# First stage of a conditioned decoder block: c spread by TensorE, whole W_ada rows, single k tiles, last tile split

## The reference

```
mod  = silu(c) @ W_ada + b_ada            # W_ada 2048 x 12288: shift1, scale1, gate1, shift2, scale2, gate2
h    = rms_norm(x, w1) * (1 + scale1) + shift1
proj = h @ W_in                           # 16 heads: 8 retention (q, k, v, gate), 8 differential (q, k, v)
...                                       # heads, W_out, second norm, MLP of width 8192, final norm
```

## Time and profile before

| | |
|---|---|
| median of 3 runs | 2376.55 us |
| the profiled execution's own time | 2377.6 us |
| its span | 2375.3 us |
| TensorE products busy | 2311.1 us, 97% |
| DVE busy | 1265.9 us, 53% |
| ScalarE busy | 751.4 us, 32% |
| GpSimd busy | 76.9 us, 3% |
| DMA queue of SP | 326.41 MB, 39.4% of 16 engines |
| mean granted clock of TensorE | 0.995 |

### The profile page before, as it was taken

The page is one execution under the profiler, slowest core; times in us unless marked ns, Lnnn a source line. Parts: engine busy times, 40 slices in busy tenths (PEclk is TensorE's granted clock), DMA queues, the critical chain, the costliest instruction groups (busy, mean ns, idle before and its releaser), DMA issues.

```text
span 2375.3 us, 28446 instructions
## 1 busy us (share of the span) xinstructions
PE 2311.1 (97%) x10328; PEld 1880.7 (79%) x10328; DVE 1265.9 (53%) x1797; ACT 751.4 (32%) x1020; POOL 76.9 (3%) x58
## 2 busy tenths in 40 slices
PE   4999999999999999999999999999999999999997
PEld 3568888878887788888888888888888888888886
DVE  7977988867676675733333333333333333333344
ACT  3233343354545422421221221221322222222332
POOL 0011110100101000000000000000000000000000
PEclk9999999999999999999999999999999999999998
DMA  9956677722222574232222222222222222222222
GB/s 377 399 204 221 230 266 248 250 94 80 80 80 79 187 275 159 86 101 97 98 98 97 93 101 96 94 95 96 97 97 97 97 97 96 99 97 95 90 95 92
DMA packets 90630, 328.25 MB, mean 138 GB/s; under 512 B 10064, under 2 KB 10576, under 8 KB 89936
## 3 DMA queue, kind: packets, MB, share of 16 engines
q1 hardware_dynamic: 89568, 326.41, 39.4%
q10 hardware_dynamic: 1008, 1.13, 0.2%
HBM read 323.31 MB, written 4.19 MB: 138 GB/s over the span
## 4 chain that ended last, share of the span: by engine, by line
issue 60%; PE 28%; DVE 9%; ACT 2%; DMA 1%; POOL 0%; SPq 0%; DVEq 0%; POOLq 0%; ACTq 0%
PE bank L436 8%; PE bank L440 8%; PE bank L437 8%; DVE ada_sb L1001 3%; DVE w_lo L994 2%; PE bank L577 1%; DVE prob L1001 1%; PE bank L543 1%; PE bank L460 1%; DMA xy<-x_t 1%; PE bank L568 0%; DMA prob<-ada 0%; ACT w_hi L719 0%; ACT L812 0%; DVE hf L1034 0%
## 5 line engine op out<-in xcount | busy, mean ns | idle before, releaser
L436 PE MATMUL bank<-act_hi,w_hi 128*128 128x512 f32 (+1 forms) x2112 | 829.5, 393 | 13.2 <-DVE act_lo L1041 4.6
L437 PE MATMUL bank<-act_lo,w_hi 128*128 128x512 f32 (+1 forms) x2112 | 820.2, 389 | 0.0
L719 ACT ACTIVATE w_hi<-raw 128x1024 fp32r<-128x1024 f32 x392 | 413.8, 1056 | 895.5 <-PE bank L440 841.6
L994 DVE TENSOR_TENSOR w_lo<-raw,w_hi 128x1024 fp32r<-128x1024 f32 x392 | 492.0, 1257 | 309.0 <-ACT w_hi L719 296.1
L440 PE MATMUL bank<-act_hi,w_lo 128*128 128x512 f32 (+1 forms) x2112 | 518.3, 387 | 0.0
L436 PEld LDWEIGHTS bank<-act_hi,w_hi 128*128 128x128 f32 x2112 | 398.1, 188 | 101.6 <-issue 17.7
L437 PEld LDWEIGHTS bank<-act_lo,w_hi 128*128 128x128 f32 x2112 | 398.1, 189 | 81.9 <-issue 1.7
L440 PEld LDWEIGHTS bank<-act_hi,w_lo 128*128 128x128 f32 x2112 | 394.5, 188 | 81.1
L436 PE MATMUL bank<-u_hi,w_hi 128*128 128x512 f32 x1024 | 399.9, 390 | 0.0
L437 PE MATMUL bank<-u_lo,w_hi 128*128 128x512 f32 x1024 | 398.6, 389 | 0.0
L1396 DVE SCALAR_TENSOR_TENSOR xy<-bank,modr,xy 128x512 f32 (+1 forms) x143 | 107.4, 751 | 418.7 <-PE bank L440 418.7
(11 more groups left out here) (140 smaller groups left out, 1115.0 us busy)
## 6 DMA issues: line engine op xcount, KB each, us to landing
raw<-weights SPq DMA_DIRECT2D x400, 512.0 KB, 3.2
ada_sb<-ada SPq DMA_DIRECT2D x172, 512.0 KB, 5.3
prob<-ada SPq DMA_DIRECT2D x20, 512.0 KB, 6.8
xy<-x_t SPq DMA_DIRECT2D x16, 512.0 KB, 6.0
out<-rows_out SPq DMA_DIRECT2D x4, 1024.0 KB, 5.9
decay_sb<-decay SPq DMA_DIRECT2D x7, 256.0 KB, 2.8
silu_c<-c_row SPq DMA_DIRECT2D x1, 1024.0 KB, 5.6
rot_sb<-rot ACTq DMA_DIRECT2D x2, 256.0 KB, 7.0
```

What stands on the lines that cost most here:

```text
L436: pe.matmul(acc, stationary, hi, start=first, stop=False)
L437: pe.matmul(acc, stationary, lo, start=False, stop=False)
L719: nc.scalar.activation(w_hi[:, w], raw[:, r], ACT.Copy).then_inc(hi_ready, 1)
L994: nc.vector.tensor_tensor(w_lo[:, w], raw[:, r], w_hi[:, w].bitcast(F32), ALU.subtract).then_inc(lo_ready, 1)
```

## The change

It touches the first stage, and the dots in all stages.

- **c** lands as one row in partition 0 on ScalarE's queue. TensorE multiplies a row of ones with its four parts of 512 into banks 0 to 3 (`spread_c`), and ScalarE takes Silu from there between squares 1 and 2, 3 and 4, 5 and 6, 7 and 8. SP's queue begins with x.
- **Dots** take whole rows of 2048 and start from the bias, in a ring of three rows (two in the heads). Only the two rows of tile 0 are still taken as halves.
- **Squares**: all 16 have their own place. TensorE sums five of them (1, 4, 7, 10, 13) itself, adding in PSUM; DVE sums the other eleven.
- **Single k tiles** instead of pairs; tile 0's hf reads the spread bank directly; in split tiles TensorE begins with the eight hi*hi products when act_hi is there, before act_lo.
- **Tile 15 is split**; its banks are finished one after another (`first_done`), so that rotations and gates wait for single banks.
- The order into head 1: four `whole_rest`, `rest_w` of chunk 16, both rotations, then the other three `whole_rest`. Both rotated halves are rounded before the five gates.
- lams and mask are loaded on SP's queue behind chunk 1, rot and decay behind chunk 16.

```diff
-NADA = 4
-NADA_1 = 6
+NADA = 2
+NADA_1 = 3
...
+PE_SQUARES = (1, 4, 7, 10, 13)
...
-WHOLE = tuple(range(1, KT, 2))
+WHOLE = tuple(range(1, KT - 1, 2))
...
# SP
-            sp.dma_start(silu_c[:], c.partition_broadcast(P128)).then_inc(c_landed, 16)
...
             for k in range(KT):
-                for a in range(4 * k, 4 * k + 4):
-                    load_ada(Count(a))
-                    if a % 4 == 2:
-                        load_raw(Count(k))
+                if k == 0:
+                    for i in range(4):
+                        load_ada_half(i)
+                else:
+                    for e in range(2):
+                        load_ada(Count(2 * k + e))
+                load_raw(Count(k))
+                if k == 1:
+                    sp.dma_start(lam_in, lams.partition_broadcast(P128)).then_inc(lam_landed, 16)
+                    sp.dma_start(mask_f, mask_in).then_inc(mask_landed, 16)
             load_raw(Count(FIRST))
+            sp.dma_start(rot_sb[:, 0], rot[0, 0]).then_inc(rot_landed, 16)
+            sp.dma_start(rot_sb[:, 1], rot[0, 1]).then_inc(rot_landed, 16)
+            sp.dma_start(decay_sb[:], decay[0]).then_inc(decay_landed, 16)
# TensorE
+                pe.wait_ge(hi_ready, made(Count(k)))
+                pe.wait_ge(act_hi_ready, k + 1)
+                for i in range(BLOCKS):
...
+                    product(i, w_hi, act_hi, start=k == 0)
+                pe.wait_ge(act_ready, SPLIT.index(k) + 1)
...
+                else:
+                    pe.wait_ge(lo_ready, made(Count(k)))
+                    for i in range(BLOCKS):
+                        product(i, w_hi, act_lo)
+                        product(i, w_lo, act_hi, stop=True).then_inc(*((first_done, 1) if i < BLOCKS - 1 else (chunk_done, 1)))
...
+            def spread_c():
+                pe.wait_ge(c_landed, 16)
+                for i in range(4):
+                    pe.matmul(bank[i][:], ones[0:1], silu_c[0:1, i * TOK:(i + 1) * TOK], start=True, stop=True)\
+                        .then_inc(c_spread, 1)
+            def first_sums():
+                for n, m in enumerate(PE_SQUARES + (None,)):
...
+                        mm = pe.matmul(ps_a[:, tb:tb + 1], ssq[:, tokens] if m is None else square_at(m)[:, tokens], inv_d[:],
+                                       start=n == 0 and tb == 0, stop=m is None, skip_group_check=True)
...
             pe.wait_ge(const_ready, 4)
-            token_sums(1)
+            spread_c()
+            first_sums()
             token_spread(1)
-            pe.wait_ge(r_all_ready, 1)
+            pe.wait_ge(silu_ready, 4)
...
-            pe.wait_ge(act_ready, KT)
+            pe.wait_ge(act_ready, len(SPLIT) + sum(k < KT // 2 for k in WHOLE))
# ScalarE
             for m in range(KT):
                 square_x(m, (x_landed[m // 2], 16))
+                if m % 2 == 1 and m < 8:
+                    i = m // 2
+                    act.wait_ge(c_spread, i + 1)
+                    nc.scalar.activation(silu_c[:, i * TOK:(i + 1) * TOK], bank[i][:], ACT.Silu).then_inc(silu_ready, 1)
+            round_w(Count(0))
+            for k in range(KT):
+                modulated_hi(0, k)
+                if k == 0:
+                    spread(1)
+                if k + 1 in SPLIT:
+                    round_w(Count(k + 1))
...
             round_rotated(1, q_hi)
+            round_rotated(2, k_hi)
             act.wait_ge(act_ready, KT)
+            for h in range(EARLY):
+                take_gate(h, bank[3 + h], first_done, 4 + h)
+            take_gate(EARLY, bank[3 + EARLY], chunk_done, FIRST)
# DVE
+            def dot1(k, e):
+                col = V_B1 + 2 * k + e
+                dot_ada(Count(2 * k + e), mod1[:, k, e:e + 1], vec[:, col:col + 1])
...
+            first_square_sums()
             dve.wait_ge(vec_landed, 16)
+            dve.wait_ge(silu_ready, 4)
+            half_dot(0, 0)
+            half_dot(0, 1)
+            scale1(0)
             token_mean(1)
+            dve.wait_ge(tok_r_ready, 1)
+            half_dot(1, 0)
+            half_dot(1, 1)
+            for k in range(KT):
+                normed(0, k)
+                if k == 0:
+                    rest_w(Count(0))
+                    modulated_rest(0, 0)
+                if k + 1 < KT:
+                    dot1(k + 1, 0)
+                if k in SPLIT and k > 0:
+                    rest_w(Count(k))
+                    modulated_rest(0, k)
+                if k + 1 < KT:
+                    dot1(k + 1, 1)
+                    scale1(k + 1)
...
+            for k in WHOLE:
+                if k < KT // 2:
+                    whole_rest(k)
             rest_w(Count(FIRST))
+            rotate_q(0, Count(FIRST), False)
+            rotate_k(0, Count(FIRST), False)
+            for k in WHOLE:
+                if k >= KT // 2:
+                    whole_rest(k)
```

More of the change, by code:

```diff
@@ L70 @@
 N_CHUNKS = C_MLP + PER_GROUP * MLP_GROUPS
-A_RET = 4 * KT
-N_ADA = 12 * KT
+A_RET = 2 * KT
 NORM_BLOCKS = ((0, 1, 2, 3), (0, 1), (2, 3), (0, 1, 2, 3))
-NORM_SQUARES = (KT, 2 * KT, 2 * KT + 1, 3 * KT + 1)
+PE_SQUARES = (1, 4, 7, 10, 13)
+DVE_SQUARES = tuple(m for m in range(KT) if m not in PE_SQUARES)
+FIRST_SUMS = len(DVE_SQUARES) - 1
+NORM_SQUARES = tuple(FIRST_SUMS + n for n in (0, KT, KT + 1, 2 * KT + 1))
 def norm_tokens(n):
@@ L374, in load_phase @@
                     load_raw(s0 + (j + 2))
-                    for _ in range(2 * slots[j]):
+                    for _ in range(slots[j]):
                         load_ada(ada_phase(h) + part)
@@ L450, in first_chunk, with product @@
             def first_chunk(k):
-                split_products([(i, bank[i][:], act_hi[:, k], act_lo[:, k], k == 0, k == KT - 1,
-                                 (act_ready, SPLIT.index(k) + 1) if i == 0 else None) for i in range(BLOCKS)], Count(k))
+                w = w_place(Count(k))
+                def product(i, weight, moving, start=False, stop=False):
+                    return pe.matmul(bank[i][:], weight[:, w, i * P128:(i + 1) * P128], moving[:, k], start=start, stop=stop)
+                pe.wait_ge(hi_ready, made(Count(k)))
@@ new lines, in first_chunk @@
+                pe.wait_ge(act_hi_ready, k + 1)
+                for i in range(BLOCKS):
+                    if k == 0 and bank[i] is ps_b:
+                        pe.wait_ge(r_all_ready, 1)
+                    product(i, w_hi, act_hi, start=k == 0)
+                pe.wait_ge(act_ready, SPLIT.index(k) + 1)
+                if k < KT - 1:
+                    for i in range(BLOCKS):
+                        product(i, w_hi, act_lo)
+                    pe.wait_ge(lo_ready, made(Count(k)))
+                    for i in range(BLOCKS):
+                        mm = product(i, w_lo, act_hi)
+                    mm.then_inc(chunk_done, 1)
+                else:
+                    pe.wait_ge(lo_ready, made(Count(k)))
+                    for i in range(BLOCKS):
+                        product(i, w_hi, act_lo)
+                        product(i, w_lo, act_hi, stop=True).then_inc(*((first_done, 1) if i < BLOCKS - 1 else (chunk_done, 1)))
@@ L1224, in diff_strips, with modulation_rest, modulation_sum @@
                 op.then_inc(strips_ready, 1)
[L1226 to L1230 removed]
+            def modulation_rest(a, part, summed):
+                if summed is not None:
+                    dve.wait_ge(modr_ready, summed)
+                dot_ada(a, partr[:, part:part + 1])
+            def modulation_sum(col, width, dots):
                 dve.wait_ge(dot_done, dots)
[L1233 to L1235 removed]
                 flat = modr[:].rearrange("p a b -> p (a b)")
@@ L1256, in head_ret @@
                     for _ in range(slots[j]):
-                        modulation_rest(ada_phase(h) + 2 * part, part)
+                        modulation_rest(ada_phase(h) + part, part, h - 1 if part == 0 and not (isinstance(h, int) and h == 1) else None)
                         part += 1
```

207 lines of the change are left out of this document (89 added, 118 removed).

## The result

The changed kernel takes 2401.22 us (median of 4 runs, 2399.76 to 2403.6) against 2376.42 for the kernel before in the same session: a ratio of 1.0102 with a 95% interval of 1.009 to 1.0113, 24.8 us slower. The forecast was 2368.2, and its range ended at 2372.5. Its profiled execution took 2399.76 us, span 2397.5.

What follows compares the result with a forecast made beforehand. DVE was taken to bound the first stage's middle, DMA queues close behind. Gates earlier -9.3, half clock +1.7, heads -0.7 sum to -8.3 us, from the median 2376.55 to 2368.2; range 2364 to 2372.5.

Steps and rivals of the forecast that it cites:

- What follows it is the same program in both kernels but for the dots: Everything after head 0's first score product was taken as unchanged except for the dots.
- Slower: Rival, 5%: TensorE waits for act_lo inside eight split tiles and drops to half clock, giving 2381.9 us.
- The signs that I had named for being wrong: Dots waiting for rows more than a few us, first product later than 32, or gates ending after 147.
- Front: Start of the first stage: first product at 29.5 instead of 33.79, 4.3 us earlier, bounds 2 and 6.
- Table: ScalarE's table switch: 1.28 us, next activation right behind it.
- The drain beside the load: The Trainium skill's extra 1.38 us per table switch; by it front and gates would together be 2.8 us later.
- Middle: First stage's k tiles: DMA becomes the bound, about 5 us of queue holes, last dot ends 123.5 instead of 129.2.
- supply binds harder: Rival, 14%: the coarse three-row ring makes the last dot end 2 to 5 us later, giving 2371.7 us.
- Back: Behind the last dot, into head 1: gates end at 143.2, 9.3 us earlier; TensorE waits 5.8, 1.7 lost to half clock.
- Heads: Whole dots and fewer small additions in the heads: 0.7 us off, bounds 0 and 1.5.

Runs made afterwards that it cites:

- a_pad64: The changed kernel with 64 unused bytes per partition behind neg_lam, so later tensors lie 64 B higher: 2380.36 us, ratio 1.0013.
- b_u192: The kernel before with 192 unused bytes ahead of u_hi, u_lo, relu and usq, no instruction changed: 2396.2 us, ratio 1.008.
- a_sq0: a_pad64 with no square summed by TensorE, VectorE adding all sixteen: 2380.06 us, ratio 1.0012.
- a_ring4: a_pad64 with a fourth place for rows of w_ada in the first stage: 2373.23 us, ratio 0.9984.
- b_u64: The kernel before with 64 unused bytes ahead of u_hi, u_lo, relu and usq, no instruction changed: 2383.61 us, ratio 1.0027.

## Why the prediction was wrong, step by step

**What the sum left out.** This is the step that failed first and cost most. "What follows it is the same program in both kernels but for the dots": the same instructions, but at other addresses. I had read the allocation of the smaller tensors as nothing. This term, put at nothing without a reason, was 21 of the miss of 33 us, and a_pad64 and b_u192 show it from both sides. None of my rivals had it. *Slower* (5%) got the direction, by a mechanism that did not happen: TensorE waited for act_lo six times, 1.4 us at most, 4.5 us in all, and the granted clock stayed at 1.00 from 40 to 130 us. The signs that I had named for being wrong all came: the first product later than 32 (32.10), waits for rows of more than a few us (5.8), gates that end after 147 (152.47).

**Front, "4.3 us earlier".** It was 1.7. The end of the spread of c was taken at 14.1 because I let the products speed up after 4.8 us of work. They did not: eight records of 0.86 to 0.9 us each, twice the 0.43, from 8.89 to 16.08. The five squares started only behind them, 40 records of 0.217 us until 24.7, 3.8 us past ScalarE's last square. The mean was closed at 26.4 instead of 23.0. The power came as priced (1.02 us); the two half dots behind it took 2.7 us instead of 2.3. a_sq0 adds that VectorE's program would have held the mean at 25.9 in any case. The start also varies by 0.6 us between executions: a_pad64, with the same code, has its first product at 31.48.

**Table.** The load took 1.28 us, and the gates began 0.94 us behind it because they waited for act_lo. Where ScalarE had nothing to wait for, as in the earlier trace rows, the next activation follows the load directly. The drain beside the load that the prediction names shows in none of these rows.

**Middle, "about 5 us of holes. Last row landed 121, its dot ended 123.5".** This is the second step that failed. Dots took 2.27 us, inside the bounds of the 2.21 priced, and the queues' full rate was as priced. The holes were larger: with places of 1 MB the windows from 20 to 40 us moved 4.9 MB where before they moved 8.1, which is 8 us of full rate. More followed: between 25 and 140 us DVE waited for rows nine times, 5.8 us in all. a_ring4 settles it: one place more and the last dot ends at 126.2. The rest to 123.5 is mostly the late front. In a_ring4 neither VectorE nor TensorE shows a wait in the middle, and a pair of tiles takes 12.6 us on each (VectorE from 88.24 to 100.84, TensorE from 89.90 to 102.50), 0.3 more than I had priced for either; which of the two sets the pace is not separated. From the first product to tile 15 TensorE needs 96.0 us (94.1 by my sum), and 29.5 + 96.0 would be 125.5, against 125.1 forecast. My rival *supply binds harder* named the mechanism, but gave it 3.5 us where it took 7 of the kernel's time.

**Back.** Right in its durations: rotate_q 6.1 us behind the last dot (6.2 forecast), the gates' end 13.2 behind rotate_q (13.5), a wait of 5.24 (5.8) and a granted clock of 0.51 behind it, from 152.5 to 156. From the last dot to the end of the gates 19.3 us were needed (19.7 forecast) instead of 23.2.

**Heads, "0.7 off".** It went the other way. From the gates' end to the first down product a_ring4 takes 894.8 us and the kernel before 891.8, 3.0 more. The scores at half clock are 1.9 of it (1.7 forecast). In TensorE's waits between 133 and 1045 us the 1.5 us for the rounded weights are gone, as hoped, but a wait is there in a_ring4 that the kernel before does not have:

```profile
PE bank L648 <- POOL sq_lo L1614: 1.7, 3, 0.7
```

A dot of 2048 columns stands longer ahead of VectorE's next step than one of 1024; that this is what delays sq_lo was not tried. The three do not add up to the whole 3.0 us; about 0.9 stays open.

In all: 2368.2 + 20 to 21 (addresses) + about 7 (ring) + about 2.5 (front) + 2 (heads) comes to about 2400; measured were 2401.2, with single times from 2399.8 to 2403.6.

## What to carry to other kernels

When a change alters the size of any tensor, compare the addresses of everything allocated after it, and keep the moving operands of long product runs a multiple of 256 B from the stationary ones, the only distance at which these runs were fast; here that was worth six times what the change proper cost. A ring's capacity is not only bytes: a place stands idle from its last read to the next landing, so when the unit of a ring doubles at equal bytes, price the hole per release and not once. And behind a tuned tail, ask for every consumer that becomes early what the engines' program order still puts ahead of it.

## What the runs showed of the hardware that I had not expected

- The pitch of fp32r products (rounded fp32 operands) of 512 columns depends on the distance between the moving and the stationary tensors, by its remainder modulo 256 B: 226.6 ns at 0 (two placements of u_hi, 256 B apart), about 229 at 64 (an estimate from b_u64's 6.6 us over 3072 products), 233.3 at 32, 128 and 192. 32 and 64 were tried in one placement each, 128 and 192 in two. In the changed kernel it was 233 ns with ScalarE and VectorE at work and with both at rest.
- TensorE's first products, 7.2 us without a gap from 8.89 on, took twice the usual 0.43 us a record to the last of them, where those of the earlier trace rows sped up after 4.8 us. The clock column of these windows reads 1.00 all the same, as it does for the slow products at 33.8 in the kernel before; so early in the span the durations tell more than that column. That it is the half clock is read from the durations alone.
- Equal waits of 2.55 us were followed by half clock (granted 0.53) in one profiled execution and by full clock (1.00) in another.
